# A hybrid decoder trunk: Fox queries and keys copied raw and normed together in slot 27, the first stick-breaking pair and the second merged turn one slot later, 384-column sums

## The reference, cut to what matters

```python
for layer in range(DEPTH):                       # DEPTH = 2, SEQ = 256, D_MODEL = 1024
    h = _rms_norm(x, attn_norm[layer])
    # h @ w_in -> u_pool, dq, dk, dv, sq, sk, sv, fq, fk, fv, f_logit, g_logit
    # pool:  running means over 2, 4, 8, 16 positions, minus u
    # diff:  q, k = rope(rms_norm(q)), rope(rms_norm(k)); two softmaxes, one minus lambda times the other
    # stick: z = q k^T / 8;  weights = exp(log_sigmoid(z) + sum of log_sigmoid(-z) over later keys), strictly causal
    # fox:   q, k = rms_norm(q), rms_norm(k); softmax(q k^T / 8 + cum(log f) differences)
    # x = x + (sum_n sigmoid(gate_n + b_gate_n) * (branch_n @ w_branch[n])) @ w_out
    x = x + _hybrid_mixer(h, ...)
    x = x + _swiglu(_rms_norm(x, ffn_norm[layer]), ...)
```

## Time and profile before

| | us |
|---|---|
| median of 3 runs | 895.01 (894.31 to 897.45) |
| the profiled execution | 895.68 |
| its span in the trace | 892.8 |
| TensorE busy | 875.3 (98%) |
| VectorE busy | 611.1 (68%) |
| ScalarE busy | 443.0 (50%) |
| GpSimd busy | 114.4 (13%) |

### The profile page before, as it was taken

How to read it: one execution, slowest core, us unless ns; L and a number is a source line. 1 busy time by engine, 2 the same in 40 slices (tenths; PEclk the granted TensorE clock), 3 DMA queues, 4 the chain that set the end, 5 groups by cost and what they waited for, 6 DMA issues and landing times.

```text
span 892.8 us, 11371 instructions
## 1 busy us (share of the span) xinstructions
PE 875.3 (98%) x4308; PEld 722.3 (81%) x4308; DVE 611.1 (68%) x902; ACT 443.0 (50%) x635; POOL 114.4 (13%) x89
## 2 busy tenths in 40 slices
PE   7998999999999999999999989999999999999998
PEld 6876888788788888888888878887887888888886
DVE  5799677777967666654478977758687676666542
ACT  5464654654445444443274645546444554444431
POOL 0553000001800010000005510000045000000000
PEclk9999999999999999999999989999999999999999
DMA  8843755475566766555555346454656466666551
GB/s 272 268 124 97 225 165 167 130 236 188 187 194 195 213 186 184 183 183 193 183 165 170 115 124 209 137 181 145 235 180 201 146 213 189 189 188 189 181 196 47
DMA packets 91014, 160.10 MB, mean 179 GB/s; under 512 B 11472, under 2 KB 17744, under 8 KB 90960
## 3 DMA queue, kind: packets, MB, share of 16 engines
q1 hardware_dynamic: 90960, 159.38, 57.3%
HBM read 158.31 MB, written 1.05 MB: 179 GB/s over the span
## 4 chain that ended last, share of the span: by engine, by line
PE 81%; DVE 13%; issue 2%; DMA 1%; ACT 1%; POOL 1%; SPq 0%; POOLq 0%; DVEq 0%; ACTq 0%
PE bulk L1591 24%; PE bulk L1595 24%; PE bulk L1592 24%; DVE w_lo L941 6%; DMA raw<-in_w_in_dram 1%; PE bankAB L1346 1%; POOL wide L667 1%; PE bankT L1486 1%; ACT w_hi L695 1%; DVE wide L1240 1%; DVE stat L1027 1%; DVE wide L1039 1%; PE bankAB L1532 1%; PE bankO L1505 1%; DVE softplus_lo L1110 0%
## 5 line engine op out<-in xcount | busy, mean ns | idle before, releaser
L941 DVE TENSOR_TENSOR w_lo<-raw,w_hi 128x1024 fp32r<-128x1024 f32 (+1 forms) x288 | 368.4, 1289 | 165.9 <-ACT w_hi L695 163.4
L695 ACT ACTIVATE w_hi<-raw 128x1024 fp32r<-128x1024 f32 (+1 forms) x288 | 299.7, 1049 | 259.7 <-PE bulk L1595 232.5
L1591 PE MATMUL bulk<-w_hi,hT_hi 128*128 128x512 f32 (+1 forms) x896 | 354.0, 395 | 3.7 <-DVE w_lo L941 3.6
L1592 PE MATMUL bulk<-w_lo,hT_hi 128*128 128x512 f32 (+1 forms) x896 | 346.8, 387 | 0.0
L1595 PE MATMUL bulk<-w_hi,hT_lo 128*128 128x512 f32 (+1 forms) x896 | 343.7, 388 | 0.0
L1591 PEld LDWEIGHTS bulk<-w_hi,hT_hi 128*128 128x128 f32 x896 | 169.3, 189 | 38.7 <-DVE w_lo L941 5.1
L1595 PEld LDWEIGHTS bulk<-w_hi,hT_lo 128*128 128x128 f32 x896 | 168.7, 189 | 34.6
L1592 PEld LDWEIGHTS bulk<-w_lo,hT_hi 128*128 128x128 f32 x896 | 169.5, 189 | 32.1
L1591 PE MATMUL bulk<-w_hi,aT_hi 128*128 128x512 f32 x176 | 68.8, 391 | 0.0
L1595 PE MATMUL bulk<-w_hi,aT_lo 128*128 128x512 f32 x176 | 68.5, 389 | 0.0
L1592 PE MATMUL bulk<-w_lo,aT_hi 128*128 128x512 f32 x176 | 68.5, 389 | 0.0
(11 more groups left out here) (240 smaller groups left out, 737.1 us busy)
## 6 DMA issues: line engine op xcount, KB each, us to landing
raw<-in_w_in_dram SPq DMA_DIRECT2D x112, 512.0 KB, 4.0
raw<-in_w_ffn_up_dram SPq DMA_DIRECT2D x80, 512.0 KB, 4.4
raw<-in_w_ffn_down_dram SPq DMA_DIRECT2D x44, 512.0 KB, 3.3
raw<-in_w_branch_dram SPq DMA_DIRECT2D x20, 512.0 KB, 3.3
raw<-in_w_out_dram SPq DMA_DIRECT2D x16, 512.0 KB, 3.2
bias<-in_b_gate_dram SPq DMA_DIRECT2D x16, 256.0 KB, 4.0
raw<-in_w_ffn_up_dram SPq DMA_DIRECT2D x16, 256.0 KB, 3.1
raw<-in_w_in_dram SPq DMA_DIRECT2D x8, 256.0 KB, 2.6
```

Source lines behind the costliest of these rows:

```text
L695: act.activation(w_hi[:, g % RING, :, 0:width], raw[:, g % RAW, :, 0:width], ACT.Copy).then_inc(hi_ready, 1)
L941: vec.tensor_tensor(w_lo[:, g % RING, :, 0:width], raw[:, g % RAW, :, 0:width], w_hi[:, g % RING, :, 0:width].bitcast(F32), ALU.subtract). ...
L1591: pe.matmul(dst, hi, whi, start=(k == ks[0]), stop=False)
L1592: pe.matmul(dst, hi, wlo, start=False, stop=False)
```

## The change

In words:

- Fox queries and keys: ScalarE copies them raw from PSUM to SBUF (`xn`), besides the values and the squares, and the squares' signal releases the PSUM item. The two norms of 256 columns on VectorE (slots 16 and 20) become one of 512 columns in slot 27, read from SBUF and written in place. GpSimd's four Fox gains wait for that.
- `sb_logs` on VectorE becomes a stage of its own, `sb_mask`, one slot behind ScalarE's part.
- Pair 0: scores 12 to 13, logs 12 to 13, mask and split 12 to 14, sums and weights 15 to 16, output 17 to 18. Pair 1: mask and split 18 to 19, the rest stays.
- In the list of slot 12 the norm of `dk` remains.
- `tr_merged` 1 and `merged_evac` 1: slot 72 to 73.
- `sb_sums`: 256 and 128 columns with the same constant matrix are one matmul of 384; the two diagonal masks of a bank are one matmul of 256 columns, also in `scores`.

The core of the diff:

```diff
 _PE = [(0, "tr_norm", "attn", 0, 1),
-       (10, "tr_ss"), (12, "sb_scores", 0), (14, "tr_qk", "dq"), (15, "sb_sums", 0),
-       (17, "sb_out", 0), (18, "sb_scores", 1), (21, "sb_sums", 1), (23, "sb_out", 1), (23, "tr_qk", "dk"),
+       (10, "tr_ss"), (13, "sb_scores", 0), (14, "tr_qk", "dq"), (16, "sb_sums", 0),
+       (18, "sb_out", 0), (18, "sb_scores", 1), (21, "sb_sums", 1), (23, "sb_out", 1), (23, "tr_qk", "dk"),
...
-        (B0 + 8, "tr_merged", 0), (O0 + 2, "tr_merged", 1),
+        (B0 + 8, "tr_merged", 0), (O0 + 3, "tr_merged", 1),
...
-       (12, "sb_logs", 0), (12, "sb_split", 0), (12, "qk_norm", "dk"), (14, "qk_evac", "dq"), (15, "sb_weights", 0),
-       (16, "svfq"), (17, "sb_evac", 0), (18, "sb_logs", 1), (18, "sb_split", 1), (20, "fkfv"), (21, "sb_weights", 1),
-       (23, "sb_evac", 1), (23, "qk_evac", "dk"), (24, "dv"),
+       (12, "qk_norm", "dk"), (13, "sb_logs", 0), (14, "sb_mask", 0), (14, "sb_split", 0), (14, "qk_evac", "dq"),
+       (16, "sb_weights", 0), (16, "svfq"), (18, "sb_evac", 0), (18, "sb_logs", 1), (19, "sb_mask", 1), (19, "sb_split", 1),
+       (20, "fkfv"), (21, "sb_weights", 1), (23, "sb_evac", 1), (23, "qk_evac", "dk"), (24, "dv"), (27, "fox_norm"),
...
-                "svfq": (normed, ("fq", t)), "fkfv": (normed, ("fk", t)), "dv": (v_ready, ("dv", t)),
+                "svfq": (squares, ("fq", t)), "fkfv": (squares, ("fk", t)), "dv": (v_ready, ("dv", t)),
...
-                    pool.wait_ge(normed, nth(normed, layer, (which, t)))
+                    pool.wait_ge(normed, nth(normed, layer, ("fox", t)))
...
+            def fox_staged(layer, which, item, c0, values):
+
+                at = 256 * ("fq", "fk").index(which)
                 for t in range(TT):
                     wait_item(act, layer, item, t)
                     src = item_bank(layer, ITEM_AT[item], t)
...
+                    act.activation(values[:, t, :], src[:, 256 - c0:512 - c0], ACT.Copy, scale=y_attn[:, t:t + 1]) \
+                        .then_inc(v_ready, 1)
+                    act.activation(xn(which, t), src[:, c0:c0 + 256], ACT.Copy)
+                    act.activation(scratch(t, SQ)[:, at:at + 256], src[:, c0:c0 + 256], ACT.Square).then_inc(squares, 1)
...
             def svfq(layer):
 
                 act.wait_ge(normed, nth(normed, layer, ("dk", 1)))
-                head_squares(layer, "fq", "svfq", 256, 256, v_s)
+                fox_staged(layer, "fq", "svfq", 256, v_s)
 
             def fkfv(layer):
-                act.wait_ge(normed, nth(normed, layer, ("fq", 1)))
-                head_squares(layer, "fk", "fkfv", 0, 256, v_f)
+                fox_staged(layer, "fk", "fkfv", 0, v_f)
...
-            def sb_logs(layer, pair):
+            def sb_mask(layer, pair):
...
-            def svfq(layer):
-                head_norm(layer, "fq", "svfq", 256, 4)
-
-            def fkfv(layer):
-                head_norm(layer, "fk", "fkfv", 0, 4)
...
+            def fox_norm(layer):
+                head_norm(layer, "fox")
...
-                        pe.matmul(b[:, 0:SEQ], sums[:, 0, :], sp[:, 0:SEQ], start=False, stop=False, skip_group_check=True)
+                        pe.matmul(b[:, 0:SEQ + P], sums[:, 0, :], sp[:, :], start=False, stop=False, skip_group_check=True)
                         pe.matmul(b[:, P:SEQ], sums[:, 1, :], sp[:, SEQ:SEQ + P], start=False, stop=False, skip_group_check=True)
-                        pe.matmul(b[:, SEQ:SEQ + P], sums[:, 0, :], sp[:, SEQ:SEQ + P], start=False, stop=False,
-                                  skip_group_check=True)
-                    pe.matmul(b[:, 0:P], masks[:, 0, :], masks[:, 2, :], start=False, stop=False, skip_group_check=True)
-                    ins = pe.matmul(b[:, SEQ:SEQ + P], masks[:, 0, :], masks[:, 2, :], start=False, stop=True, skip_group_check=True)
+                    diagonal = b.rearrange("p (k q) -> p k q", k=4)[:, 0:3:2, :]
+                    ins = pe.matmul(diagonal, masks[:, 0, :], masks[:, 2:3, :].broadcast_to([P, 2, P]),
+                                    start=False, stop=True, skip_group_check=True)
```

More of the change, by code:

```diff
@@ L216 @@
         _SV += [(LAST[("branch", _j, _n)] + 1, "branch", _j, _n)]
-_SV += [(B0 + 8, "merged_evac", 0), (O0 + 2, "merged_evac", 1),
+_SV += [(B0 + 8, "merged_evac", 0), (O0 + 3, "merged_evac", 1),
         (F0 - 3, "residual", "out", 0, 0), (F0 - 3, "gain", "ffn", 0, 0),
@@ L385, in xn @@
         def xn(which, t):
-            at, width = {"dq": (2048, 512), "dk": (0, 512), "fq": (512, 256), "fk": (768, 256)}[which]
+            at, width = {"dq": (2048, 512), "dk": (0, 512), "fq": (512, 256), "fk": (768, 256), "fox": (512, 512)}[which]
             return wide[:, t, at:at + width]
@@ L439, in build @@
         squares = signal("squares", [(w, t) for w in ("dq", "dk", "fq", "fk") for t in range(TT)])
-        normed = signal("normed", [(w, t) for w in ("dq", "dk", "fq", "fk") for t in range(TT)])
+        normed = signal("normed", [(w, t) for w in ("dq", "dk", "fox") for t in range(TT)])
         rotated = signal("rotated", [(w, t) for w in ("dq", "dk", "fq", "fk") for t in range(TT)])
@@ L717, in norm_evac, with head_squares @@
                          bank["ABTO"[2 * t + b]].rearrange("p (k q) -> p k q", k=4))
-            def head_squares(layer, which, item, c0, width, copy_to=None):
+            def head_squares(layer, which):
+                for t in range(TT):
+                    wait_item(act, layer, which, t)
+                    act.activation(scratch(t, SQ), item_bank(layer, ITEM_AT[which], t), ACT.Square).then_inc(squares, 1)
+            def fox_staged(layer, which, item, c0, values):
+                at = 256 * ("fq", "fk").index(which)
                 for t in range(TT):
@@ L735, in qk_norm @@
                     act.wait_ge(sumsq["attn"], nth(sumsq["attn"], layer, (1, 1)))
-                head_squares(layer, which, which, 0, 512)
+                head_squares(layer, which)
             def fox_forget(layer):
@@ L899, in _ @@
                           qk_norm=qk_norm, lambda_sums=lambda_sums, lambdas=nothing, pf=pf, sb_split=sb_split, maxima=nothing,
+                          sb_mask=nothing, fox_norm=nothing,
                           fox_forget=fox_forget, qk_evac=qk_evac, cum_evac=nothing, pool_evac_a=pool_evac_a,
@@ L1013, in norm_evac, with head_norm @@
                          hT[0][:, 4 * b:4 * b + 4, t * P:(t + 1) * P])
-            def head_norm(layer, which, item, c0, heads):
-                width, n = heads * HD, TT * heads
+            def head_norm(layer, which):
+                heads, n = 8, TT * 8
                 if which == "dq":
@@ L1025, in head_norm @@
                 for t in range(TT):
-                    vec.wait_ge(squares, nth(squares, layer, (which, t)))
+                    vec.wait_ge(squares, nth(squares, layer, ("fk" if which == "fox" else which, t)))
                     last = vec.reduce_sum(m_[:, t * heads:(t + 1) * heads],
-                                          scratch(t, SQ, width).rearrange("p (h d) -> p h d", d=HD), AX_X)
+                                          scratch(t, SQ).rearrange("p (h d) -> p h d", d=HD), AX_X)
                 last.then_inc(vec_step, 1)
@@ L1037, in head_norm @@
                 for t in range(TT):
-                    src = item_bank(layer, ITEM_AT[item], t)[:, c0:c0 + width].rearrange("p (h d) -> p h d", d=HD)
-                    vec.tensor_tensor(xn(which, t).rearrange("p (h d) -> p h d", d=HD), src,
+                    src = xn("fox", t) if which == "fox" else item_bank(layer, ITEM_AT[which], t)
+                    vec.tensor_tensor(xn(which, t).rearrange("p (h d) -> p h d", d=HD), src.rearrange("p (h d) -> p h d", d=HD),
                                       y_[:, t * heads:(t + 1) * heads].unsqueeze(2).broadcast_to([P, heads, HD]),
@@ L1046, in qk_norm @@
             def qk_norm(layer, which):
-                head_norm(layer, which, which, 0, 8)
+                head_norm(layer, which)
+            def fox_norm(layer):
+                head_norm(layer, "fox")
             def pf_items(layer):
@@ L1281, in _ @@
                           fox_forget=fox_forget, qk_evac=qk_evac, cum_evac=cum_evac, pool_evac_a=nothing,
-                          pool_evac_b=pool_evac_b, ss=nothing, ss_evac=ss_evac, sb_logs=sb_logs, svfq=svfq,
-                          sb_weights=nothing, sb_evac=sb_evac, fox_evac=fox_evac, fkfv=fkfv, dv=nothing,
+                          pool_evac_b=pool_evac_b, ss=nothing, ss_evac=ss_evac, sb_logs=nothing, svfq=nothing,
+                          sb_mask=sb_mask, fox_norm=fox_norm,
+                          sb_weights=nothing, sb_evac=sb_evac, fox_evac=fox_evac, fkfv=nothing, dv=nothing,
                           softmax=softmax, probs_evac=nothing, pv_evac=pv_evac, diff_norm=diff_norm,
@@ L1476, in scores @@
                                 False, False)
```

(5 more changed lines are left out.)

4 lines of the change are left out of this document (removed).

## The result

The changed kernel takes 905.89 us (median of 4 runs, 905.37 to 907.18); the kernel before, timed with it, 894.85 (4 runs). The ratio is 1.0133, interval 1.0104 to 1.0162: 1.3% slower. The forecast was 908.0, range 896 to 917. The profiled execution took 905.37 us, its span is 903.6.

A forecast was written before the change was run, and what follows sets the result against it. TensorE, busy 98% of the span, was taken as the bound, through its waits, work and clock. Gains of 15.1 us against losses of 28.1 gave net +13.0 on 895.68, 908.7, or 908 us for the median; range 898 to 916.5, stated also as 896 to 917.

The forecast's parts named there:

- Slot 16: TensorE waits for pair 0's late mask work on VectorE; loss 10.3 us, bounds 6.5 and 11.9.
- Slot 31: Joint norm in slot 27 delays forget logits, exponentials and head-2 scores; loss 3.6 us a layer, 7.2 together.
- The clock: A spell at 1.2 GHz behind each of four new waits; loss 10 us, bounds 6.8 and 13.6.
- Slots 20 and 21: Fox norms leave pair 1's way: gains 1.2, 6.2 and 3.9 (clock) us; 0.6 lost to a remaining slot-21 wait.
- Slot 12: Scores of pair 0 go to slot 13, when their operands are ready; gain 1.1 us over both layers.
- The merged turn: Second merged turn one slot later, when GpSimd is done; gain 2.2 us.
- The joined matmuls: Fewer matmuls in the sums gain 0.6 us, joined masks lose 0.1; net gain 0.5, bounds -0.5 and +1.0.
- only slot 16: Rival: only slot 16 waits, since the Fox norm finds idle time on VectorE; 896 us, chance 0.1.
- only slot 27: Rival: only slot 27 waits, VectorE reaching slot 12 four microseconds sooner; 893 us, chance 0.07.
- The rival on the other side: Faster: VectorE relieved of one Fox norm a layer, chains covered, nearly the whole gain stands; 880.5 us, chance 0.09.

The follow-up runs named there:

- the rotation held back: Changed kernel with GpSimd's rotation of the differential keys starting only when the low part of pair 0 is there; 896.04 us.
- the first two experiments: Changed kernel with the joint Fox norm in slot 21 instead of 27: 894.23 us; changed kernel with pair 0 in its old slots: 894.04 us.
- the third experiment: Changed kernel with both edits, pair 0 in its old slots and the joint Fox norm in slot 21; 880.52 us, ratio 0.9857.
- the best kernel: Changed kernel with pair 0 in its old slots and the joint Fox norm in slot 21; 880.52 us.
- pair 0 back: Changed kernel with pair 0 in its old slots (scores, logs, mask and split 12, sums 15, output 17); 894.04 us, ratio 0.9996.
- the small parts: Kernel before with only the second merged turn a slot later and the joined matmuls; 889.45 us, ratio 0.9953.

## Why the prediction was right

The forecast said slower by 13.0 us on the profiled execution; the profiles differ by 905.37 - 895.68 = 9.7 us, and the medians by 11.0. The interval of the ratio is 9.3 to 14.5 us, so 13.0 lies inside it, and what follows on the missing 2 us is read from one trace of each kernel. Time beyond the bulk products (from the start of the last bulk product before a stage to the start of the next one, less 0.23, added over the trace) rose from 89.3 to 100.9 us, 11.6; the span grew by 10.8, and the difference lies outside these steps. By steps:

- **Slot 16, right.** Forecast 5.7 us of wait in layer 0 and 4.6 in layer 1, 10.3 together; measured 5.48 and 4.69, 10.2. The mask work was expected at 60 us and began at 59.4. The value for the work beside GpSimd's rotation was put between its bounds, 1.9 us a layer, and the three operations were longer by 0.9, 1.1 and 0.2, 2.2 in all. The total was right and its division was not: I called 6.5 of it the place in the queue, though that sum held the two splits at 3.62 us, the length they have beside GpSimd. Without the rotation the wait is 3.2 us, not 6.5.
- **Slot 31, right in size, the size worked out on the wrong path.** Forecast 3.6 us a layer, measured 3.7. But the 3.6 were worked out for the scores, which were to wait for the exponentials of head 1. They did not: the exponentials were done by 118.5 and the scores began at 119.75. Only the cumulative sum waited, for the forget logits; without that wait TensorE would have come to the scores at about 114.8 and waited there instead. These had been ready 2.5 us before TensorE came (108.80 to 111.34), and came 8.5 us later (117.27), while TensorE came 2.1 us later. The two paths run close together; that the size came out has some luck in it. The wait of ScalarE for the forget logits was 8.5 us, 8 had been forecast. The joint norm was expected at 104 and began at 106.33, 2.3 us later, as TensorE itself was some 2 us later.
- **The clock, right in the sum.** Four spells, 10 us forecast, 10.4 measured (3.2 + 2.8 + 2.6 + 1.7). The sum owes something to luck: 2.5 us was the middle of two values, and with the rotation held back the same waits of 3.7 us in slot 31 were followed by 3.41 us of low clock in both layers, not by 6.83 and 3.41.
- **Slots 20 and 21, right.** Forecast 1.2 for slot 20, measured 1.1. For slot 21, 6.2 and 3.9 less 0.6 were forecast, with 0.3 for its matmuls 9.8; measured were 4.11 + 5.22 + 3.5 of slow products before and 1.57 twice after, 9.7. The rest of 0.3 us a layer is in the trace as well. The cause named for it, the Fox norms, is sufficient but not alone: by the run with pair 0 moved alone, the wait in slot 16 would have brought the same.
- **Slot 12, right.** 1.1 forecast, 1.2 measured.
- **The merged turn, a little low.** 2.2 forecast, 2.6 measured: 2.10 to 0.80 in each layer, the wait and some of the matmuls behind it.
- **The joined matmuls, undervalued.** 0.5 us net was forecast. A call of the sums went from 57.92 to 59.46, 1.54 us, to 85.47 to 86.75, 1.28 us: 0.26 us, four times, 1.0 (forecast 0.6). The masks, which I had put at a loss of 0.1, gained 0.8 us (a call of scores from 1.03 to 0.97, and 1.06 to 1.01 in the Fox heads). Together 1.8. This is the mis-sized term, and its 1.3 us are the largest part of the 2 us between 13.0 and 11. The forecast set a rule of TensorE: Matmul & The Clock Gate (the Trainium skill, section Back-to-back issue gap) beside it, by which joining some fifty matmuls would give 0.13 us. It left out that the section calls this the gap of an isolated matmul, which under-counts short matmuls that come with weight loads: 56 ns by the rule and about 81 measured, for 128 columns. This trace agrees with the reservation and not with the rule: the sixteen matmuls of a call, 128 or 256 columns each with a weight load, took 1.54 us, 96 ns each.

The forecast's losses came to 28.1 us, of which 0.6 for slot 21. Against the other 27.5 stand 17.6 us of waiting and 10.4 of slow clock, 28.0 (10.2 + 5.9 in slot 16, 7.4 + 4.5 in slot 31). So the losses were as forecast, and what made the change less slow than forecast are the gains. The rivals of the first kind ("only slot 16", "only slot 27") are what the first two experiments built: 896 and 893 forecast, 894.2 and 894.0 measured. The rival on the other side, 880.5 us when VectorE's queue has the masks early and the norm in a pause, is the third experiment, with 880.5.

SBUF — State Buffer (the Trainium skill, section Who interferes with whom) has a VectorE instruction with two SBUF inputs and a GpSimd instruction that reads SBUF exclude each other for whole instructions. The trace agrees as far as it goes: the lengthening of single operations by 0.2, 0.9 and 1.1 us, beside GpSimd's of 0.7 to 1.9, is compatible with that, and the two masks ended at 61.66 and 63.07, 0.3 us after GpSimd operations that ended at 61.38 and 62.78. It does not prove it.

## What to carry to other kernels

In a list of work bound to slots by hand, the position that counts is the engine's own time, not the slot's number: a stage set a slot later on TensorE can become two splits and a norm later on an engine that is behind. Before moving a heavy operation, look in the engine's order of time for a pause and for the first consumer of what stands behind the new place; the same 5 us norm cost some 12 us in slot 27 and nothing that a trace shows in slot 21. And look at what another engine starts at the end of a moved operation: here seven of ten microseconds of waiting came from GpSimd's rotation running beside the chain, not from the order itself.

## What the runs showed of the hardware

- The clock behind a wait isn't settled by the wait's length. 2.28 us of idle time was followed by a spell at 1.2 GHz in the kernel before, 2.29 us was followed by none with the rotation held back. Spells came as 3.41 or 6.83 us, and the longer one went with waits of 2.3 as well as of 5.5 us (layer 1 of the kernel before, layer 0 of the changed one). What decides between them stays open.
- A spell in the warm-up, beginning at 11 to 13 us, is in some profiled executions and not in others: none in three (the kernel before, the changed one, pair 0 back), 3.41 us in three (the best kernel among them), 6.83 us in four. By half of TensorE's work in it, it costs 1.7 to 3.1 us. No edit moves anything in the first 30 us, and executions of one kernel differ too: those of the kernel before had mean granted clocks of 0.990 to 1.000, and took 889.9 us at 0.998 and 898.5 at 0.990. The clock is not all of it, for one took 893.0 at 1.000. So a few microseconds between two single executions say little.
- A VectorE operation with two SBUF operands of 256 columns took 0.42 us alone and 1.30 to 1.48 beside GpSimd's rotation, over three times as long; the split of 1024 columns took 1.8 instead of 1.2. The operation of 768 columns with one of its two inputs in PSUM took 0.94 beside the rotation and 0.95 without it.
- A matmul joined to its neighbour saved 0.04 to 0.05 us in the sums (0.26 to 0.33 us for six matmuls and their weight loads; 0.33 in the kernel before with the small parts, where no wait stands before the call) and 0.03 in the masks (0.8 us for 24).
- ScalarE's raw copies, 8 more instructions in the whole kernel and 2.0 us more busy time, left no mark on any of TensorE's waits shown above.
